# Every second one of the first 32 expert-row products made by GpSimd and summed by ScalarE

## The reference, cut to what matters

```python
def peer_ffn(x, norm_g, w_query, sub_keys, u_table, v_table):
    h = rmsnorm(x, norm_g).reshape(T, D)
    q = (h @ w_query).reshape(T, PEER_HEADS, 2, PEER_DHALF)
    s = jnp.einsum('thpd,hpnd->thpn', q, sub_keys)
    vals, idx = lax.top_k(s, PEER_TOPK)                       # 16 of 128, twice per head
    cand = vals[:, :, 0, :, None] + vals[:, :, 1, None, :]
    top_s, pos = lax.top_k(cand, PEER_TOPK)                   # 16 of the sums
    experts = jnp.take_along_axis(cidx, pos, axis=-1)
    gates = jax.nn.softmax(top_s, axis=-1)
    # per token t and chosen expert e
    act = jax.nn.gelu(jnp.einsum('td,ted->te', hb, ue), approximate=False)
    return jnp.einsum('te,ted->td', gb * act, ve)
```

## Time and profile before

| what | value |
|---|---|
| median of 3 timed runs | 1583.55 us (1582.47 to 1584.18) |
| the profiled execution: its time, its span | 1587.31 us, 1585.5 us |
| TensorE / VectorE / ScalarE / GpSimd busy | 1551.8 / 1091.9 / 295.6 / 462.4 us |
| DMA | 531.83 MB, mean 335 GB/s |
| VectorE dot products (L1349), 192 | 232.9 us, 1227 ns each |
| GpSimd fetch issues (L582), 384 | 410.6 us |
| ScalarE Gelu of a pair (L828), 128 | 56.0 us, 438 ns each |
| GpSimd candidate sums of 4 heads (L536), four operations | 1.18 us |

### The profile page before, as it was taken

How to read it: one execution, slowest core, us unless ns; L and a number is a source line. 1 busy time by engine, 2 the same in 40 slices (tenths; PEclk the granted TensorE clock), 3 DMA queues, 4 the chain that set the end, 5 groups by cost and what they waited for, 6 DMA issues and landing times.

```text
span 1585.5 us, 30461 instructions
## 1 busy us (share of the span) xinstructions
PE 1551.8 (98%) x11510; PEld 1454.8 (92%) x11510; DVE 1091.9 (69%) x2333; ACT 295.6 (19%) x632; POOL 462.4 (29%) x477
## 2 busy tenths in 40 slices
PE   8999999999999999999999999999999999999998
PEld 6778899999999999899977688999999999998998
DVE  5578899678846874544388778996788478644443
ACT  6385410100000000000066753001000000000000
POOL 0002044333433343333100020443333324433330
PEclk9999999999999999999999999999999999999999
DMA  6455599999999999999854264999999999999996
GB/s 245 162 147 190 178 351 358 385 402 408 409 409 409 371 400 409 409 410 410 340 182 151 80 200 172 348 367 388 399 408 409 409 408 403 406 409 409 409 410 248
DMA packets 150925, 531.83 MB, mean 335 GB/s; under 512 B 18736, under 2 KB 22080, under 8 KB 150464
## 3 DMA queue, kind: packets, MB, share of 16 engines
q1 hardware_dynamic: 88416, 321.43, 52.9%
q0 software_dynamic: 57056, 204.60, 33.2%
q10 hardware_dynamic: 5376, 4.81, 1.2%
HBM read 527.41 MB, written 1.06 MB: 333 GB/s over the span
## 4 chain that ended last, share of the span: by engine, by line
PE 86%; DMA 7%; DVE 4%; issue 2%; ACT 1%; ACTq 0%; POOL 0%; DVEq 0%; SPq 0%; POOLq 0%
PE ps L1940 34%; PE ps L1882 29%; PE ps L1694 4%; DMA raw<-stream 3%; PE ps L1709 3%; PE ps L1711 3%; PE ps L1710 3%; DMA big<-u_rows,own 2%; PE ps L1692 2%; PE ps L1893 2%; DMA big<-stream 1%; PE ps L1859 1%; PE ps L1829 1%; DVE big L1349 1%; PE ps L1691 1%
## 5 line engine op out<-in xcount | busy, mean ns | idle before, releaser
L1447 DVE SCALAR_TENSOR_TENSOR big<-big,own_act 128x1024 f32<-128x1024 f32 x192 | 246.5, 1284 | 208.1 <-PE ps L1940 111.2
L1349 DVE SCALAR_TENSOR_TENSOR big<-big 128x1024 f32<-128x1024 f32 x192 | 232.9, 1227 | 125.8 <-DMA big<-u_rows,own 94.3
L582 POOL DMA_INDIRECT big<-u_rows,own x192 | 209.2, 1089 | 338.3 <-DVE big L1349 320.5
L582 POOL DMA_INDIRECT big<-v_rows,own x192 | 201.4, 1049 | 342.0 <-DVE big L1447 321.0
L1940 PE MATMUL ps<-big 128*128 (+1 forms) x2048 | 294.9, 302 | 4.9 <-issue 0.2
L1940 PE MATMUL ps<-big,raw 128*128 (+1 forms) x2048 | 292.3, 301 | 3.7
L1940 PEld LDWEIGHTS ps<-big 128*128 128x128 f32 x2048 | 280.5, 190 | 16.6 <-issue 15.6
L1940 PEld LDWEIGHTS ps<-big,raw 128*128 128x128 f32 x2048 | 280.2, 190 | 12.1 <-issue 11.1
L1882 PE MATMUL ps<-big 128*128 128x160 f32 x2048 | 285.8, 300 | 0.4 <-DMA big<-stream 0.2
L1882 PE MATMUL ps<-big,raw 128*128 128x160 f32 x2048 | 285.1, 300 | 0.5 <-DMA raw<-stream 0.4
L1882 PEld LDWEIGHTS ps<-big 128*128 128x128 f32 x2048 | 279.9, 190 | 1.3 <-DMA big<-stream 0.9
(11 more groups left out here) (254 smaller groups left out, 1286.4 us busy)
## 6 DMA issues: line engine op xcount, KB each, us to landing
raw<-stream SPq DMA_DIRECT2D x353, 512.0 KB, 4.1
big<-stream SPq DMA_DIRECT2D x256, 512.0 KB
big<-u_rows,own POOLq DMA_INDIRECT x192
big<-v_rows,own POOLq DMA_INDIRECT x192
big<-keys ACTq DMA_DIRECT2D x2, 1024.0 KB, 7.8
big<-row_copy ACTq DMA_DIRECT2D x6, 256.0 KB, 5.5
x<-x_in SPq DMA_DIRECT2D x1, 1024.0 KB, 5.6
big<-big POOLq DMA_DIRECT2D x4, 256.0 KB, 3.4
```

Source lines behind the costliest of these rows:

```text
L582: pool.indirect_dma_start(out=fetched[:, b, :], out_offset=None, in_=table, in_offset=bass.IndirectOffsetOnAxis(ap=own[:, 0, k:k + 1].bitc ...
L1349: dve.scalar_tensor_tensor(out=row, in0=row, scalar=1.0, in1=own_h[token_class(k)], op0=ALU.mult, op1=ALU.mult, accum_out=own_act[:, k:k + ...
L1447: dve.scalar_tensor_tensor(out=out_, in0=row, scalar=own_act[:, k:k + 1], in1=out_, op0=ALU.mult, op1=ALU.add).then_inc(row_used, 1)
```

## The change

Of u rows 0 to 31 of a layer the even ones leave VectorE. GpSimd multiplies such a row with the token tile into one of two tiles `product`, and ScalarE sums it with a Copy that accumulates into `own_act`; its 16 sums stand behind the Gelus of pairs 6, 7, 9, 10, 12 and so on to 28. VectorE keeps the odd ones, now 16 instead of 20 dot products in the routing, and from w = 48 it goes on with row 32 instead of 20. GpSimd's queue is in order: products, fetches, the second `own_indices` (before fetch 8) and the third `candidates` (before fetch 18).

```diff
+        product = [area(12288, D), area(13312, D)]
-        DOTS_TO_INDEX, DOTS_TO_SEARCH, DOTS_ROUTING = 4, 10, 20
+        INDEX_AT, CANDIDATES_AT, DOTS_ROUTING = 8, 18, 32
+        POOL_DOTS, SUMS_PAIR = DOTS_ROUTING // 2, 6
+        DVE_ROWS = 2 * FETCHES - POOL_DOTS
+        def on_pool(k):
+            return k < DOTS_ROUTING and k % 2 == 0
+        def dve_rows(k):
+            return k - min((k + 1) // 2, POOL_DOTS)
             def fetch(l, table, f):
-                b, n = f % FETCH_RING, 2 * FETCHES * l + f
-                if n >= FETCH_RING:
-                    pool.wait_ge(row_used, n - FETCH_RING + 1)
+                b, before = f % FETCH_RING, f - FETCH_RING
+                if before < 0:
+                    if l > 0:
+                        pool.wait_ge(row_used, DVE_ROWS * l + before + 1)
+                elif on_pool(before):
+                    pool.wait_ge(product_ready, POOL_DOTS * l + before // 2 + 1)
+                else:
+                    pool.wait_ge(row_used, DVE_ROWS * l + dve_rows(before + 1))
+            def row_product(l, k):
+                n, b = POOL_DOTS * l + k // 2, k % FETCH_RING
+                pool.wait_ge(row_landed[b], 16 * ((2 * FETCHES * l + k) // FETCH_RING + 1))
+                if n >= 2:
+                    pool.wait_ge(product_summed, n - 1)
+                pool.tensor_tensor(product[n % 2], fetched[:, b, :], own_h[token_class(k)], ALU.mult
+                                   ).then_inc(product_ready, 1)
...
+                pool.wait_ge(own_h_ready, 2 * (l + 1))
                 for f in range(FETCHES):
                     if f == FETCH_RING:
                         candidates(l, 1)
-                    if f == DOTS_TO_INDEX + FETCH_RING:
+                    if f == INDEX_AT:
                         own_indices(l, 1)
-                    if f == DOTS_TO_SEARCH + FETCH_RING:
+                    if f == CANDIDATES_AT:
                         candidates(l, 2)
+                    if f >= FETCH_RING and on_pool(f - FETCH_RING):
+                        row_product(l, f - FETCH_RING)
...
+                SUM_PAIRS = [SUMS_PAIR + 3 * k // 2 for k in range(POOL_DOTS)]
+                def row_sum(k):
+                    n = POOL_DOTS * l + k
+                    act.wait_ge(product_ready, n + 1)
+                    act.activation(product[n % 2], product[n % 2], ACT.Copy, accum_out=own_act[:, 2 * k:2 * k + 1]
+                                   ).then_inc(product_summed, 1)
...
+                    if pair in SUM_PAIRS:
+                        row_sum(SUM_PAIRS.index(pair))
-                act.wait_ge(row_used, 2 * FETCHES * l + FETCHES)
+                act.wait_ge(row_used, DVE_ROWS * l + dve_rows(FETCHES))
+                act.wait_ge(product_summed, POOL_DOTS * (l + 1))
...
-                dots(2)
+                dots(1)
                 whole(second16(1, 4))
-                dots(DOTS_TO_INDEX - 2)
+                dots(1)
                 indices(1)
...
                 for s in range(2):
                     expand(0, s, 0, SLOTS)
-                    dots(2)
+                    dots(1)
```

More of the change, by code:

```diff
@@ L336, in program @@
         row_used = sem("row_used")
+        product_ready = sem("product_ready")
+        product_summed = sem("product_summed")
         own_gelu = sem("own_gelu")
@@ L1354, in dots @@
                 def dots(count):
-                    for k in range(rows_done[0], rows_done[0] + count):
-                        row_dot(k)
-                    rows_done[0] += count
+                    for _ in range(count):
+                        while on_pool(rows_done[0]):
+                            rows_done[0] += 1
+                        row_dot(rows_done[0])
+                        rows_done[0] += 1
                 indices(0)
@@ L1444, in row_add @@
                     row = row_landing(FETCHES + k)
-                    dve.wait_ge(row_used, 2 * FETCHES * l + FETCHES + k)
+                    dve.wait_ge(row_used, DVE_ROWS * l + dve_rows(FETCHES + k))
                     out_ = own_out[token_class(k)]
@@ L1450, in gate_rows @@
                 def gate_rows():
-                    dve.wait_ge(row_used, 2 * FETCHES * l + FETCHES)
+                    dve.wait_ge(row_used, DVE_ROWS * l + dve_rows(FETCHES))
                     for c in range(2):
@@ L1969, in ffn @@
                         pe.wait_ge(fold_ready, 3)
-                        pe.wait_ge(row_used, 2 * FETCHES * (l + 1))
+                        pe.wait_ge(row_used, DVE_ROWS * (l + 1))
                         for c in range(2):
```

## The result

The changed kernel takes 1628.76 us (median of 4 runs, 1623.50 to 1630.61) against 1583.87 us (1582.47 to 1585.21) in the same session: ratio 1.0271, 95% interval 1.0258 to 1.0284. It is 44.9 us slower. The prediction had the direction, but said 1594 and at most 1614, and of the 44.9 us it had forecast 10.4.

What follows compares the result with a forecast made beforehand. After unit 70 DMA transfers were taken to bound a layer; second weights 18 us late less 12.8 given back lose 5.2 per layer, +10.4 in all: 1597.7 in the profile's terms, 1594 us against the median 1583.55, range 1576 to 1614.

Steps and rivals of the forecast that it cites:

- Unit 70 is 18 us late: Start of TensorE's second weights in layer 0: 366.3 instead of 348.4 us, because VectorE reaches slots and one-hots late.
- a sign of being right: Unit 70 at 360 to 370 us, beside TensorE, GpSimd and VectorE waiting at the places named.
- this exclusion: VectorE and GpSimd wait for each other: a VectorE subtraction takes 1.23 us alone, 2.65 and 3.09 beside GpSimd products.
- 10 x 1.28 = 12.8 us given back: After unit 70: 48 rows used by then, not 38, each saving 1.28 us of later transfers per layer.
- The sign named for being wrong: A layer's end that does not follow from unit 70's date and the transfers left.
- the balance: After unit 70 a layer ends when its transfers are through: 334 rows and units x 1.28 = 427.5 us.
- The sum: Whole kernel: 18 - 12.8 = 5.2 us lost per layer, +10.4 us for two layers.
- Places of the waits: TensorE at unit 48 and the second weights (some 10 us), GpSimd at the third candidates, VectorE at rows 15, 19, 23.
- the slot turn in time for unit 56: End of the routing in layer 0: slots ready at 323, in time for TensorE's unit 56 at 323.3.
- The gap in the DMA is filled: Rival, chance 0.24: 12 more routing rows use idle DMA from 210 to 315 us; at most 17 us gained, 1566.5.
- Products twice as expensive: Rival, chance 0.14: GpSimd's products and VectorE lock each other out throughout, 3.38 us each and upper landing; +32, 1616.
- The Trainium skill's rule: Exclusive lock for the whole instruction: each of 16 products could add its 2.4 us to VectorE at `expand` or dot products.

Runs made afterwards that it cites:

- e1_tiny: The changed kernel, but GpSimd multiplies only 32 of 1024 columns and ScalarE sums the token tile; waits and fetches stay: 1602.36 us, ratio 1.0114.
- e3_cand20: The changed kernel with the third candidates asked for before fetch 20 instead of 18: 1618.01 us, ratio 1.0209.
- e8_dve32: The kernel before with 32 rows in the routing, all multiplied by VectorE, no product on GpSimd: 1605.61 us, ratio 1.0133.
- e6_later: The changed kernel with no row behind the routing's 32 due before unit 66: 1622.69 us, ratio 1.0240.
- e2_warm: The changed kernel with dummy matmuls where TensorE would wait, to keep its clock up: 1627.82 us, ratio 1.0280.

## Why the prediction was right or wrong, point by point

- **"Unit 70 is 18 us late": mis-sized.** It is 25.5, and past the 360 to 370 us named as a sign of being right (layer 1: 1182.83 against 1138.38, of which 18.8 were there when the layer's feed-forward began, at 1002.24 instead of 983.47: 25.7). By dates: `top_ready` 304.4 for 302, unit 38 late as well (a wait of 3.1 us; 0.7 had been forecast, and like it the 3.1 lie hidden behind the wait at unit 48), unit 48 at 307.2 for 305.9, slots 330.2 for 323, second weights 373.9 for 366.3. Of the 7.6 us by which the second weights are later than forecast, 2.4 were there at `top_ready` (row 19's dot product alone was 2.7 too long), 4.8 arose between it and the slots: 25.8 us, not 21. In that stretch three steps of VectorE's took 3.26, 3.19 and 1.93 us where 1.23, 1.15 and 1.23 stand without a product: 4.8 us. The prediction had named this exclusion and then put it into the products' duration, 2.7 us, where it was not to be found (2.40): it lengthens VectorE's operation, and hardly GpSimd's. (That 2.40 held was luck: of the four products in the earlier trace rows the median is 3.19.)
- **"10 x 1.28 = 12.8 us given back": wrong, and with 14.3 us of the missing 31.1 nearly as large an error as the date (15.2).** A sum of transfers is a bound only as long as it is the largest. TensorE's own rest of a layer is 429 to 430 us; four kernels with 48 rows used there (after, e1_tiny, e3_cand20, e8_dve32) have 428.3 to 430.2 in both layers. The kernel before stood some 8 us above this in layer 0 and 3 to 5 in layer 1, so 8.3 and 3.0 were all that came back. The kernel before could have warned: TensorE is busy for 432.0 of 437.4 us and for 428.9 of 433.0 in the windows above, so little is to be had beyond some 5 us (layer 0 gave back more, as the busy time itself fell from 432.0 to 427.0); the earlier trace rows end at 500 us, and layer 1 was not looked at. The sign named for being wrong, an end that does not follow from unit 70's date and the transfers left, is what came. e6_later shows that the balance has the right size where transfers are the larger.
- **The sum.** Predicted +10.4. Second weights 7.5 + 7.7 more, give-back 4.5 + 9.8 less, 1.6 between the layers, which nothing here explains: +31.1, together the 41.5 by which the two profiles differ. The medians differ by 44.9; the other 3.4 are the profiled execution of the kernel before, which stood that much above its median.
- **Places of the waits: right.** Unit 48 behind the exponentials, the second weights, the third candidates with a product behind them, VectorE at row 19: all four are in the trace. GpSimd waited 8 us at the candidates for a forecast of 7, and VectorE 10.8 us for row 19. What stood ahead of the routing's end (the slot turn in time for unit 56) failed by 4.3 us.
- **"The gap in the DMA is filled" (0.24): refuted for 32 rows.** A few rows gain: 22 rows give 3.4 us, and from 210 to 315 us the DMA engines move 384 GB/s instead of 376, which fits this rival. From 24 on the one-hots are too late. That 32 rows alone, without any product on GpSimd, cost 21.7 us (e8_dve32) was in no rival.
- **"Products twice as expensive" (0.14)** gave 1616, itself outside the range, and was the nearest, but by durations that did not occur: products took 2.40, not 3.38. The slots came near its upper end all the same (330 for 334).
- **The Trainium skill's rule** ("SBUF — State Buffer", section "🔬 SBUF: two separate sides": a VectorE operation with two SBUF inputs and a GpSimd one exclude each other): this trace agrees, 3.90 and 3.26 us beside a product, 1.23 and 1.22 in e1_tiny, where the product is 32 columns wide. By that rule up to 2.4 us would be added for each of 16 products, an estimate of 38 a layer; the part that reached the second weights is 11 us (373.9 against 363.0 in e1_tiny), by exclusion and by the products' own time in the queue together.

So the 2.71% are two nearly equal parts: asking for 32 rows in the routing (1.33% in e8_dve32, 1.14% in e1_tiny, which keeps the new queue), and GpSimd's full products (the other 1.38 to 1.57%). The 0.62% of the third candidates can't be put into one of them: e1_tiny has the wait still (7.83 us), e8_dve32 has 3.25 us like the kernel before. What is open: how much of the products' part in the time is exclusion and how much the 2.4 us in the ring's cycle; e1_tiny removes both, and its dates in layer 0 split only the slots, 7.8 us of 14.7 for VectorE's longer operations behind row 19.

## What to carry to other kernels

Before counting a saving that a bound gives back, work out the next bound below it, for every layer: here it was some 3 to 8 us away and not 12.8. Work put ahead of a due date has to be priced at the last date of that chain (the one-hots), not at the first with cover (the slots): where rows land at a fixed spacing behind it, most of the lateness is passed on. And an engine that takes over half of an item's work in an in-order queue takes over its waits too: look at what is queued in front.

## What was not expected of the hardware

- A product on GpSimd mostly kept its 2.34 to 2.40 us beside VectorE (the longest of 32 took 2.99), and VectorE's two-input operation beside it grew from 1.23 to 3.90 (f32) and from 1.22 to 3.26 (f16). The loss was nearly all on one side here, while in the earlier trace rows the median is 3.19 and the longest 3.38. It was on VectorE's side even where VectorE's row starts first: row 19's dot product starts at 284.77, the product at 285.21, and the dot product ends 1.1 us after it.
- Row fetches and unit loads share the DMA engines evenly: a row lands every 2.57 us behind the routing, with 407 GB/s in all. The window is of the kernel before:

```profile
300.00:318.00 18.00, 18.00 (x136) 18.00 (x135) 8.63 (x14) 1.75 (x4) 6.85 (x8) 1.00 1.03 407
```

- Behind waits of 3 to 6 us TensorE's next units were slower (64 matmuls 10.63 instead of 8.86 us), where the granted clock is 0.88 on the mean (276 to 290 us); behind the wait of 5.89 us it is 0.50, the lower of its two levels of 2.4 and 1.2 GHz (370 to 374 us). e2_warm kept it nearly up and gained nothing.
